# Half A's depthwise convolution without TensorE: three chunks on ScalarE and GpSimd, five on VectorE, and one pair of half B moved behind pw2

## The reference

```python
h = rmsnorm(x, g);  u = h @ pw1_w + pw1_b          # 1024 -> 2048
a, gate = jnp.split(u, 2, axis=-1)
u = a * jax.nn.sigmoid(gate)
u = depthwise causal convolution of u along the tokens, 31 taps per channel, + dw_b
u = jax.nn.silu(layernorm(u, ln_g, ln_b))
x = x + u @ pw2_w + pw2_b
x = x + swiglu(rmsnorm(x, ffn_norm_g))
```

## Time and profile before

| | us |
|---|---|
| median of 3 runs | 2307.05 |
| lowest, highest | 2306.18, 2307.67 |
| the profiled execution | 2304.78 |
| its span | 2303.0 |
| mean granted clock of TensorE in it | 0.994 |

### The profile page before, as it was taken

One profiled execution on the slowest core, in us unless ns is written; L12 is line 12 of the kernel. 1 busy time (PEld: TensorE's weight loads), 2 busy tenths in 40 slices (PEclk: granted clock), 3 DMA queues, 4 the chain that ended last, 5 costly groups with the idle time before them and its releaser, 6 DMA issues.

```text
span 2303.0 us, 27743 instructions
## 1 busy us (share of the span) xinstructions
PE 2245.9 (98%) x10517; PEld 1822.7 (79%) x10517; DVE 1673.9 (73%) x2617; ACT 903.6 (39%) x1603; POOL 68.7 (3%) x51
## 2 busy tenths in 40 slices
PE   7999989999999999999999999999999999999998
PEld 6885768888888888887777777878788888877887
DVE  6998589999666634345677777774778888977875
ACT  5221532222344423223455555564443233324443
POOL 0000000000000000002111111000000000000000
PEclk9999999999999999999999999999999999999999
DMA  4110223333333333332111111121023333338642
GB/s 142 47 37 19 74 74 92 101 90 99 92 95 97 95 101 89 103 90 84 37 38 38 37 38 38 62 60 44 28 78 95 98 113 99 113 101 305 202 155 110
DMA packets 287666, 202.13 MB, mean 88 GB/s; under 512 B 9045, under 2 KB 254126, under 8 KB 287534
## 3 DMA queue, kind: packets, MB, share of 16 engines
q1 hardware_dynamic: 287534, 200.36, 28.4%
HBM read 174.37 MB, written 25.95 MB: 87 GB/s over the span
## 4 chain that ended last, share of the span: by engine, by line
PE 89%; DVE 8%; ACT 1%; issue 1%; DMA 1%; SPq 0%; DVEq 0%; ACTq 0%
PE ps L2306 27%; PE ps L2308 27%; PE ps L2307 26%; PE ps L2444 3%; PE ps L2289 3%; DVE cacc L1655 2%; DVE cvA L1655 2%; PE ps L2402 1%; DVE sc L1906 1%; DVE Wl L1580 0%; ACT sc L1305 0%; PE ps L2361 0%; DVE Sl L1821 0%; PE ps L2371 0%; DVE rstd L1593 0%
## 5 line engine op out<-in xcount | busy, mean ns | idle before, releaser
L2306 PE MATMUL ps<-Sh,Wl 128*128 128x512 f32 x1616 | 655.5, 406 | 16.7 <-DVE Sl L1743 7.2
L2308 PE MATMUL ps<-Sh,Wh 128*128 128x512 f32 x1616 | 632.4, 391 | 0.0
L2307 PE MATMUL ps<-Sl,Wh 128*128 128x512 f32 x1616 | 631.7, 391 | 0.0
L2306 PEld LDWEIGHTS ps<-Sh,Wl 128*128 128x128 f32 x1616 | 305.0, 189 | 94.9 <-issue 33.2
L2308 PEld LDWEIGHTS ps<-Sh,Wh 128*128 128x128 f32 x1616 | 304.4, 188 | 65.8
L2307 PEld LDWEIGHTS ps<-Sl,Wh 128*128 128x128 f32 x1616 | 305.2, 189 | 59.5 <-issue 3.4
L1580 DVE TENSOR_TENSOR Wl<-raw,Wh 128x1024 fp32r<-128x1024 f32 (+1 forms) x178 | 213.4, 1199 | 87.3 <-ACT Wh L1092 86.0
L1092 ACT ACTIVATE Wh<-raw 128x1024 fp32r<-128x1024 f32 (+1 forms) x178 | 183.2, 1032 | 153.0 <-DMA raw<-in_ffn_w_dram 126.0
L2306 PE MATMUL ps<-G0h,Wl 128*128 128x512 f32 x352 | 138.6, 394 | 0.0
L2308 PE MATMUL ps<-G0h,Wh 128*128 128x512 f32 x352 | 137.0, 389 | 0.0
L2307 PE MATMUL ps<-G0l,Wh 128*128 128x512 f32 x352 | 137.0, 389 | 0.0
(11 more groups left out here) (279 smaller groups left out, 3862.9 us busy)
## 6 DMA issues: line engine op xcount, KB each, us to landing
raw<-in_ffn_w_dram SPq DMA_DIRECT2D x130, 512.0 KB, 3.8
raw<-in_pw_w_dram SPq DMA_DIRECT2D x32, 512.0 KB, 4.0
raw<-in_ffn_w_dram SPq DMA_DIRECT2D x32, 448.0 KB, 3.7
draw<-in_ffn_w_dram SPq DMA_DIRECT2D x55, 256.0 KB, 4.0
raw<-in_ffn_w_dram SPq DMA_DIRECT2D x36, 256.0 KB, 4.2
graw<-t_dram SPq DMA_DIRECT2D x36, 256.0 KB, 4.2
graw<-g_dram SPq DMA_DIRECT2D x33, 256.0 KB, 4.5
g_dram<-st SPq DMA_DIRECT2D x27, 256.0 KB, 2.0
```

The lines of the kernel that those rows point to most:

```text
L2306: pe.matmul(dst, ll, rh, start=start, stop=False)
L2307: pe.matmul(dst, lh, rl, start=False, stop=False)
L2308: return pe.matmul(dst, lh, rh, start=False, stop=stop)
```

## The change

Chunks 0, 1, 3, 5 and 7 of half A are convolved by VectorE, as before but with the accumulators of chunks 3, 5 and 7 in PSUM banks 6 and 7; the last even tap and the closing add write to `cvA` in SBUF. Chunks 2, 4 and 6 are convolved by ScalarE, which makes each tap's product (the first two straight into the two accumulators, the other 29 into a ring of four tiles `tap`), and GpSimd, which adds each of the 29 to one of the accumulators, and then the two together. ScalarE's products are written out between its other work in slices of mostly nine. The diagonals and TensorE's part are gone. TensorE's order becomes: the pairs through (4, B), then (5, A), (6, A), (7, A), the means of chunks 0 to 3, (6, B), the means of chunks 4 to 7, (7, B), the sum of squares, pw2, and (5, B), whose two weight blocks (AGAIN, AGAIN + 1) are loaded and split a second time, in banks 6 and 7. The sum for the RMSNorm stands in the middle of (5, B)'s first block. The weight blocks of pairs use banks by turn of pairs and no longer by half. At the start, TensorE transposes the first three row blocks of x before the parameters and the fourth one behind them. The ring slot of the feed-forward blocks is shifted by two, and the first two of them are split earlier.

```diff
+BEHIND = LATE - 1
+PAIRS1 = [(n, hf) for n in range(BEHIND) for hf in (LA, LB)] + [(n, LA) for n in range(BEHIND, KC)] + \
+    [(n, LB) for n in range(LATE, KC)] + [(BEHIND, LB)]
+CONV_V, CONV_G = (0, 1, 3, 5, 7), (2, 4, 6)
+IN_BANKS = CONV_V[2:]
+LOW_AT = {(0, 16): 4, (0, 24): 5, (1, 16): 6, (1, 24): 7, (3, 16): 10, (3, 21): 11, (5, 2): 14, (5, 7): 15}
+GLU_AT = {(0, 8): (0, LB), (0, 28): (1, LA), (1, 8): (1, LB), (1, 20): (2, LA), (3, 14): (3, LB), (3, 30): (4, LA),
+          (5, 13): (6, LA), (5, 28): (7, LA), (7, 13): (6, LB)}
+TAP_BUFS = 4
...
@@ gpsimd
+            for m, n in enumerate(CONV_G):
+                o = cvA[:, n, :]
+                for i in range(2, CW):
+                    dst = cg[:, :] if i % 2 else o
+                    pool.wait_ge(p_ok, m * CW + i + 1)
+                    if i >= 4:
+                        pool.wait_ge(cg_s, m * (CW - 2) + i - 3)
+                    pool.tensor_tensor(dst, dst, tap[:, tap_slot(m, i), :], ALU.add).then_inc(cg_s, 1)
+                pool.wait_ge(cg_s, (m + 1) * (CW - 2))
+                pool.tensor_tensor(o, o, cg[:, :], ALU.add).then_inc(cg_ok, 1)
...
@@ scalar
+            def taps(n, i0, i1):
...
+                    if i == 0:
+                        act.wait_ge(u_ok, pair(n, LA) + 1)
+                        act.wait_ge(zero_ok, 1)
+                        act.activation(cvA[:, n, :], src, ACT.Identity, bias=col("dw_b", n), scale=wj).then_inc(p_ok, 1)
+                    elif i == 1:
+                        if m:
+                            act.wait_ge(cg_ok, m)
+                        act.activation(cg[:, :], src, ACT.Copy, scale=wj).then_inc(p_ok, 1)
+                    else:
+                        k = m * (CW - 2) + i - 2
+                        if k >= TAP_BUFS:
+                            act.wait_ge(cg_s, k - TAP_BUFS + 1)
+                        act.activation(tap[:, tap_slot(m, i), :], src, ACT.Copy, scale=wj).then_inc(p_ok, 1)
...
+            taps(4, 18, 27)
+            gate(6, LA)
+            pad(6)
+            taps(4, 27, CW)
+            taps(6, 0, 6)
+            gate(7, LA)
+            pad(7)
+            taps(6, 6, 15)
+            gate(6, LB)
+            taps(6, 15, CW)
...
+            hi(AGAIN + 1)
             act.activation(spare, eps, ACT.Sqrt)
+            hi(F0A.block0)
             root(1, LA, SUM_F0A)
...
+                if n == 3:
+                    hi(F0A.block0 + 1)
+            act.wait_ge(mm, F0A.result0 - 1)
+            act.wait_ge(acc_ok, squares_added(SUM_F0A, KC - 1))
+            act.activation(sq[:, 0, :], ps[:, 6, :], ACT.Sigmoid, bias=col("pw1_b", KC + BEHIND)).then_inc(sig_ok, 1)
...
@@ vector
+                two = (ps[:, 6, :], ps[:, 7, :]) if hf == LA and n in IN_BANKS else (o, cacc[:, :])
...
-                    dve.scalar_tensor_tensor(dst, src, wj, dst, ALU.mult, ALU.add).then_inc(conv_s, 1)
+                    dve.scalar_tensor_tensor(o if i == CW - 1 else dst, src, wj, dst, ALU.mult, ALU.add).then_inc(conv_s, 1)
...
             add_square(SUM_LN_A, KC - 1)
+            glu(KC - 1, LB)
             recip(0, LA)
...
-            glu(LATE, LB)
             for n in range(KC):
                 ln_low(LA, n)
...
-            glu(CONV_PE, LB)
...
+                if n == KC - 2:
+                    lo(AGAIN)
             add_square(SUM_F0A, KC - 1)
+            lo(AGAIN + 1)
+            lo(F0A.block0)
             recip(1, LA)
...
+                if n == 5:
+                    lo(F0A.block0 + 1)
...
@@ tensor
-            pe.wait_ge(vec_ev, 3)
-            for t in range(4):
+            for t in range(3):
                 pe.wait_ge(xn_ok, t + 1)
...
+            for n in range(4):
                 mean(LA, n)
             pw1_pair(LATE, LB)
+            for n in range(4, KC):
+                mean(LA, n)
+            pw1_pair(KC - 1, LB)
             sum_up(SUM_LN_A)
-            pw1_pair(CONV_PE, LB)
...
-            sum_up(SUM_F0A)
+
+            def sum_beside(k):
+                if k == 4:
+                    sum_up(SUM_F0A)
+
+            for what in range(2):
+                dense(AGAIN + what, 6 + what, Sh[:, LB], Sl[:, LB], KC, cv_ok, len(CONV_V), None if what else sum_beside)
```

More of the change, by code:

```diff
@@ L947, in _ @@
                 load(PW2A + n, cols(pw2, n))
+            load(AGAIN, cols(pw1, KC + BEHIND))
+            load(AGAIN + 1, cols(pw1, BEHIND))
             ffn(F0A)
@@ L1137, in pad @@
                 act.activation(upB[:, n, 0:PAD], upA[:, n, HT:UP], ACT.Copy).then_inc(pad_ok, 1)
[L1139 to L1160, removed]
+            def taps(n, i0, i1):
+                m = CONV_G.index(n)
+                for i in range(i0, i1):
+                    j = i // 2 + (TAPS0 if i % 2 else 0)
+                    wj = dw[:, j * KC + n:j * KC + n + 1]
+                    src = upA[:, n, j:j + HT]
+                    if i == 0:
[11 more added lines that the diff above has]
+                        act.activation(tap[:, tap_slot(m, i), :], src, ACT.Copy, scale=wj).then_inc(p_ok, 1)
@@ new lines, in _ @@
+            hi(2)
+            gate(0, LA)
+            hi(3)
+            gate(0, LB)
+            pad(0)
+            hi(4)
+            act.wait_ge(lam_s, 2)
+            act.activation(lexp, lsum, ACT.Exp).then_inc(lam_e, 1)
+            gate(1, LA)
+            x_copies(0)
+            hi(5)
+            gate(1, LB)
+            x_copies(4)
+            pad(1)
+            hi(6)
+            gate(2, LA)
+            x_copies(8)
+            hi(7)
+            taps(2, 0, 10)
+            gate(2, LB)
@@ new lines, in _ @@
+            x_copies(12)
+            pad(2)
+            hi(8)
+            hi(9)
+            taps(2, 10, 19)
+            gate(3, LA)
+            taps(2, 19, CW)
+            gate(3, LB)
+            pad(3)
+            hi(10)
+            hi(11)
+            gate(4, LA)
+            pad(4)
+            taps(4, 0, 9)
+            gate(4, LB)
+            hi(12)
+            hi(13)
+            taps(4, 9, 18)
+            gate(5, LA)
+            hi(14)
+            hi(15)
+            pad(5)
@@ L1180, in _ @@
                 ln_square(LA, n)
-            gate(LATE, LB)
+            gate(KC - 1, LB)
             act.activation(spare, eps, ACT.Sqrt)
@@ L1665, in _ @@
             glu(0, LA)
-            for n in range(CONV_PE):
+            for n in CONV_V:
+                if n == 3:
+                    glu(2, LB)
+                    lo(8)
+                    lo(9)
+                    glu(3, LA)
+                if n == 5:
+                    glu(4, LB)
+                    lo(12)
+                    lo(13)
+                    glu(5, LA)
                 for i in range(CONV_OPS):
-                    if i == 0 and n == 2:
+                    if (n, i) == (1, 0):
                         dve.wait_ge(lam_e, 1)
@@ L2336, in pw1_results @@
                     else:
-                        free, value = (u_ok if what else sig_ok), pair(n - 1, hf) + 1
-                    dense(gate_block(n) + what, 2 * hf + what, Sh[:, hf], Sl[:, hf], KC, free, value, ready)
+                        free, value = (u_ok if what else sig_ok), pair(n, hf) - 1
+                    dense(gate_block(n) + what, 2 * (pair(n, hf) % 2) + what, Sh[:, hf], Sl[:, hf], KC, free, value, ready)
                     ready = None
```

167 lines of the change are left out of this document (83 added, 84 removed).

## The result

The changed kernel takes 2313.83 us (median of 8 runs, 2309.27 to 2315.39), the kernel before 2306.91 beside it (8 runs, 2305.95 to 2307.98): a ratio of 1.0028, 95% interval 1.0019 to 1.0037. The forecast was 2289, the range 2284 to 2301, and a gain over the kernel before; the change is a small loss of 7 us. The profiled execution took 2314.35 us, its span is 2312.5, its mean granted clock 0.986.

A forecast was written before the change was run, and what follows sets the result against it. TensorE, 98% busy, was taken to bound the kernel, with GpSimd last in the changed convolution. 2304.78 less 21.1 by pw2's end plus 3.1 behind it gave 2286.8; with 2.27 for the median, 2289 us, range 2284 to 2301.

The forecast's parts named there:

- my 2286.8: Whole kernel: forecast for the profiled execution, 2304.78 less 21.1 gained by pw2's end plus 3.1 behind pw2.
- The start: TensorE's start, transposes ahead of the parameters: first product at 16.1 in place of 19.19, 3.1 us gained.
- VectorE's taps in PSUM: VectorE's convolution chunks: taps cost the same in PSUM, except a chunk's first two at 0.66 us, +0.4 a chunk.
- GpSimd, r = 1.05: GpSimd's additions in pw1: 1.05 us each, slices have slack, 35 additions from 161.3, last sum at 199.7.
- VectorE done at 197.7: VectorE's convolution: chunk 5 from 148.9 to 173.7, chunk 7 with 2.1 us of waiting, ending at about 197.7.
- The reciprocal at 216.6: LayerNorm behind pw1: means wait for GpSimd, (7, B) ends at 214.7, then the sum, reciprocal at 216.6.
- 57.0 us from the reciprocal to pw2's end: LayerNorm chain and pw2: last Sl 18.2 us behind the reciprocal, pw2 ending 57.0 behind it, at 273.6.
- (5, B) behind pw2, 3.1 us: Behind pw2: (5, B) fills a 10.2 us wait, but the longer chain ends the first feed-forward block 3.1 us later.
- GpSimd slower: Rival on GpSimd's additions: at 1.40 us each, 35 take 12.3 us more, 2301; chance 0.16 for 2294 to 2302.
- no gain, about 2306: Rival case in pw1: additions above 1.2 outlast a pair, late gates cost some 5 us more; chance 0.05.
- Both signs: Among the signs of a wrong forecast in pw1: GpSimd additions above 1.2 us, and waits ahead of gates.
- the two engines shutting each other out: Rival on VectorE and GpSimd: 58 taps each wait 1.05 us for an addition, 2350; chance 0.06 with other losses.

The follow-up runs named there:

- The early split: Changed kernel with pw2's first two weight blocks rounded and their remainders taken ahead of the mean, not in the LayerNorm chain: 2309.86 us, ratio 1.0011.
- The run with the repeated column: Changed kernel with the second operand of GpSimd's 87 tap additions replaced by a column repeated along the row: 2294.12 us (one run).
- The bank run: Changed kernel with the accumulators of VectorE's chunks 3, 5 and 7 back in SBUF instead of PSUM banks: 2353.6 us (one run).

## Why the prediction was wrong

The profiled execution took 2314.35 us, 27.55 over my 2286.8 for it. (The medians are 24.8 apart: I had added 2.27 us from execution to median, and after the change the median lies 0.5 under the profiled one.) The step that failed is GpSimd's, the third below. By my own steps:

- **The start**: 16.1 forecast, 15.98 measured. Right. But I had carried the 3.1 us on to the convolution's end, and in the kernel before all but 0.1 is given back by then.
- **VectorE's taps in PSUM**: 0.66 from start to start, and 0.73 and 0.65 for a chunk's first two, where I had 0.66. Right.
- **GpSimd, r = 1.05**: wrong, in two ways. First the size: 1.25, because the row I took it from repeats its second operand. Second, what I concluded from it, "the slices have slack: nine additions are 9.5 us in the 10.88 of a pair", and that GpSimd resumes at 161.3 with 35 additions to go. Nine at 1.25 are 11.3, more than a pair, so sigmoids stand behind taps; VectorE's products wait for them; and GpSimd's next chunk waits for a product. At 161.13 it has not 35 but 45 additions to go. Ten more are 12.5 us, 0.2 on each of the other 35 are 7.0, two that met remainders 2.0: 21.5, against 220.4 - 199.7 = 20.7 (its last additions run at 1.23).
- **VectorE done at 197.7**: 211.4. This follows from the step above: chunk 5 begins at 159.68 in place of 148.9, and two sigmoids are waited for 1.1 and 3.1 us, where I had counted 2.1 for one pair: 12.9 of the 13.7.
- **The reciprocal at 216.6**: 237.86, 21.3 late, of which 20.7 are GpSimd's. TensorE's wait ahead of the means is 28.1 and not 13.5.
- **57.0 us from the reciprocal to pw2's end**: 60.3. I took this from the earlier trace rows, where the pair (7, B) stood in between and hid the first block's remainder; I moved the pair and did not ask what it had covered: TensorE now waits 14.67 us ahead of pw2, where I had 9. The early split gave 55.3.
- **(5, B) behind pw2, 3.1 us**: 6.0. The layer starts 12.1 behind pw2's end in place of 10.2; six short waits for Sl (2.9 in place of 0.3) and 2.1 for G0l follow, less 0.6, which I put down to the better clock (1.00 in place of 0.78 from 297 to 320) and did not measure. That VectorE may fall behind there I had named, but for half B's means and not for the layer's own remainders.

The sum closes: 21.3 + 3.3 + 2.9 = 27.5, with the 0.6 as what was left over. The run with the repeated column tests it: with additions as short as I had forecast, the reciprocal is at 218.81 and the time 2294, so some 20 us are GpSimd's additions; of the 7 us left, 5 stand behind the reciprocal.

Of the rivals, "GpSimd slower" named the cause and even the point from which it would bite (above 1.2 gates are late), but priced it at "no gain, about 2306" at r = 1.40. At 1.25 it cost more than that. Both signs that I had named for it came: additions above 1.2 and waits ahead of gates. I had added late sigmoids as some 5 us, as if each were late once. They feed back: late sigmoid, late product, late chunk on GpSimd, later taps. Of the two engines shutting each other out I had priced only the accumulators, and of the remainders only that they slow an addition, not that one may itself be held for 9.81 us. The remainders keep two SBUF inputs, and seven of them met additions. The bank run's 2353.6 lies next to my 2350 by luck: I had put 61 us on 2289, and it is 40 on 2314.

On this the Trainium skill ("SBUF — State Buffer", section "Summary: rules for kernel authors") says that the second of the two to issue blocks fully until the first finishes. For GpSimd the trace agrees (1.29 becomes 2.28, 1.0 more beside a remainder of 1.1). For VectorE it doesn't hold as an upper bound: in those 9.81 us not one addition goes by but seven, so a VectorE instruction with two SBUF inputs may stay out while additions follow one another.

## What to carry to other kernels

Price an operation from a row with the same form of operands, not only the same size: a repeated column as second operand made GpSimd a fifth faster. Then add up what the helper engine has to do from its first start to the time at which it is needed: at 1.05 us GpSimd had 20 us of slack for pauses between 84.6 and 199.7, at 1.25 it had 2.6. When a helper engine is given a chain through a small ring, whatever stands behind the chain in the feeding engine's order runs at the helper's pace; once a slice takes longer than the period that it is to fit in, the lateness feeds back into the helper's own inputs, so that its price can't be had from one slice. And when a block of work is moved, ask what it covered at the place that it leaves.

## What the runs showed of the hardware

An addition of GpSimd's on 128x512 float32: 1.25 us a step with two full operands, 1.00 with a repeated column as second operand (1.04 long), 0.70 on 256 columns (0.73 long); from 1.25 and 0.70 I estimate a fixed part of 0.15. Beside VectorE taps with their accumulator in SBUF, both engines go at 1.70 us a step (VectorE alone 0.66). With VectorE's accumulator in PSUM both keep their own pace, 0.66 and 1.25. A VectorE remainder beside additions took mostly 1.2 to 2.7 us, 4.2 in four runs, once 4.82 and once 9.81. These long ones ended where GpSimd had a gap, ahead of its closing addition or of a late product; shorter ones got in between additions that followed without one. What decides between the two, no run here shows.
